# A list of further expert tiles, and the second attention entered tile by tile

## What is computed

```python
for i in range(DEPTH):
    hl = xl * (1.0 + sc1_l) + sh1_l
    # i == 0: window attention on 256 tokens and 256 of context; i == 1: differential attention
    xl = layer_norm(DEEPNORM_ALPHA * xl + g1_l * al, ln_attn_g[i], ln_attn_b[i])
    hl2 = xl * (1.0 + sc2_l) + sh2_l
    # the experts: 512 tokens in layer 0 (with context), 256 in layer 1
    xl = layer_norm(DEEPNORM_ALPHA * xl + g2_l * yl, ln_ffn_g[i], ln_ffn_b[i])

def moe_ffn(h, ...):          # 16 experts in 4 groups, two experts of one group for each token
    for e in range(N_EXPERTS):
        y = (jax.nn.silu(h @ w_gate[e]) * (h @ w_up[e])) @ w_down[e]
        out = out + gates[:, e:e + 1] * y
```

## Time and profile before

| | us |
|---|---|
| median of 3 runs | 2689.21 (2688.8 to 2693.2) |
| the profiled execution, its time | 2687.47 |
| its span in the profile | 2685.6 |
| PE busy | 2363.7 (88%) |
| DVE busy | 1625.8 (61%) |
| ACT busy | 1332.1 (50%) |
| POOL busy | 123.0 (5%) |

### The profile page before, as it was taken

How to read it: one execution, slowest core, us unless ns; L and a number is a source line. 1 busy time by engine, 2 the same in 40 slices (tenths; PEclk the granted TensorE clock), 3 DMA queues, 4 the chain that set the end, 5 groups by cost and what they waited for, 6 DMA issues and landing times. The chain is left out here.

```text
span 2685.6 us, 29338 instructions
## 1 busy us (share of the span) xinstructions
PE 2363.7 (88%) x11416; PEld 1886.5 (70%) x11416; DVE 1625.8 (61%) x2313; ACT 1332.1 (50%) x2010; POOL 123.0 (5%) x118
## 2 busy tenths in 40 slices
PE   8999889999999979899889887999938976999963
PEld 6887667888888758788766575777726754877741
DVE  5556245655555535555624577898866477888832
ACT  5555344655555534555324514777722443777720
POOL 0001000000000000000010000000012000000001
PEclk9999889999999979999899997999969987999986
DMA  7664455665665544666324637999953115999963
GB/s 250 235 234 157 173 219 174 206 219 207 230 220 188 173 157 147 222 233 216 116 70 167 217 130 258 378 377 380 360 181 126 49 49 172 376 375 384 380 235 120
DMA packets 175534, 588.04 MB, mean 219 GB/s; under 512 B 14960, under 2 KB 23600, under 8 KB 143632
## 3 DMA queue, kind: packets, MB, share of 16 engines
q1 hardware_dynamic: 153120, 503.95, 53.0%
q10 hardware_dynamic: 15632, 57.87, 5.4%
q0 software_dynamic: 6624, 24.12, 2.4%
HBM read 538.62 MB, written 47.28 MB: 218 GB/s over the span
## 5 line engine op out<-in xcount | busy, mean ns | idle before, releaser
L315 DVE TENSOR_TENSOR LO<-RAW,HI 128x1024 fp32r<-128x1024 f32 x558 | 659.8, 1220 | 222.6 <-ACT HI L301 220.9
L301 ACT ACTIVATE HI<-RAW 128x1024 fp32r<-128x1024 f32 x558 | 568.5, 1053 | 366.6 <-PE PS L373 191.5
L371 PE MATMUL PS<-HI,FR 128*128 128x512 f32 (+2 forms) x1808 | 699.1, 387 | 36.9 <-DVE LO L315 16.3
L373 PE MATMUL PS<-HI,FR 128*128 128x512 f32 (+2 forms) x1808 | 691.4, 382 | 0.0
L372 PE MATMUL PS<-LO,FR 128*128 128x512 f32 (+2 forms) x1808 | 690.6, 382 | 0.0
L301 ACT ACTIVATE HI<-RAW,SM 128x512 fp32r<-128x512 f32 (+2 forms) x576 | 360.4, 681 | 309.5 <-PE PS L373 159.5
L317 DVE SCALAR_TENSOR_TENSOR LO<-RAW,SM,HI 128x512 fp32r<-128x512 f32 (+2 forms) x576 | 378.8, 709 | 212.1 <-ACT HI L301 212.0
L371 PEld LDWEIGHTS PS<-HI,FR 128*128 128x128 f32 x1808 | 344.9, 191 | 110.6 <-DVE LO L315 20.8
L373 PEld LDWEIGHTS PS<-HI,FR 128*128 128x128 f32 x1808 | 344.3, 190 | 66.2
L372 PEld LDWEIGHTS PS<-LO,FR 128*128 128x128 f32 x1808 | 345.1, 191 | 62.5
L435 ACT ACTIVATE FR<-PS 128x512 fp32r<-128x512 f32 x224 | 122.4, 587 | 236.7 <-PE PS L416 218.6
(11 more groups left out here) (296 smaller groups left out, 2275.9 us busy)
## 6 DMA issues: line engine op xcount, KB each, us to landing
RAW<-in_w_ffn_in SPq DMA_DIRECT2D x88, 1024.0 KB, 5.2
RAW<-in_w_gate SPq DMA_DIRECT2D x68, 1024.0 KB, 7.8
RAW<-in_w_up SPq DMA_DIRECT2D x68, 1024.0 KB, 7.3
RAW<-in_w_down SPq DMA_DIRECT2D x64, 1024.0 KB, 8.5
RAW<-in_w_ada SPq DMA_DIRECT2D x48, 1024.0 KB, 4.9
RAW<-in_w_ffn_out SPq DMA_DIRECT2D x44, 1024.0 KB, 5.1
RAW<-in_w_in SPq DMA_DIRECT2D x44, 1024.0 KB, 5.1
YD<-CN ACTq DMA_DIRECT2D x24, 1024.0 KB, 5.1
```

Source lines behind the costliest of these rows:

```text
L301: e.activation(HI[:, i % NSPLIT, c], raw_of(j)[:, c], ACT.Copy, scale=1.0 if g is None else g).then_inc(*hi_done.up())
L315: e.tensor_tensor(LO[:, i % NSPLIT, c], raw_of(j)[:, c], hi, ALU.subtract).then_inc(*lo_done.up())
L371: e.matmul(o, h, hi[:, j, :], start=first and k + j == 0, stop=False)
L373: x = e.matmul(o, ll, hi[:, j, :], start=False, stop=end)
```

## The change

The further tiles come from a list. `dve_list` finds, in every layer, the up to eight pairs of expert and level whose tile is needed, in ascending order, and writes four things for each: whether it is there (`CNT` 0 to 7), its expert (8 to 15), its first row in `YD` (16 to 23), and the token indices of its places (`IDX` 72 to 79). `further` is a nest of at most `MORE` = 7 conditions in layer 0 and 3 in layer 1. The loads of weights and the store address memory by a register. "The tile before it" is now the one before it in the list. SP's wait for PE moves into the taken branch. The list comes after `dve_weights`, the maximum over the experts is gone, and the counts are no longer converted in `dve_route`.

At the end of layer 0, the norms of tiles 2 and 3 move before the further tiles. ACT and DVE split the first parts of `wqkv_b_2` there too, before the additions. DVE modulates tile 0 before the gate and addition of tile 1, and PE turns and projects tile 0 before it turns tile 1. The additions of tiles 2 and 3 move behind the second part of block 0 and the third of block 1 on DVE, and before `hi_parts` of block 0 on ACT.

```diff
+        MORE = [7, 3]
+        def dve_list(e, q, l):
+            s, n = f"m{l}", 16 * (X_TILES[l] - 1)
+            cf, tokens = x_s2[:, 32:48], PS[bank[f"{s} tokens"]][:, 16:16 + n]
+            key, col, step, top = x_y1[:, 0:n], x_y1[:, 64:72], x_y1[:, 72:88], x_y1[:, 96:104]
+            same = x_y1[:, 512:512 + 8 * n].rearrange("p (i c) -> p i c", i=8)
+            over = x_y1[:, 128:128 + n]
+            for j in range(1, X_TILES[l]):
+                e.tensor_scalar(over[:, 16 * j - 16:16 * j], cf, float(P * j), None, ALU.is_gt).then_inc(*dve.up())
+            e.tensor_scalar(key, C["iota"][:, 16:16 + n], -1.0, 64.0, ALU.mult, ALU.add).then_inc(*dve.up())
+            q.wait_ge(*dve.last())
+            e.tensor_tensor(key, key, over, ALU.mult).then_inc(*dve.up())
+            q.wait_ge(*dve.last())
+            e.max(top, key).then_inc(*dve.up())
+            q.wait_ge(*dve.last())
+            e.tensor_scalar(col, top, -1.0, 64.0, ALU.mult, ALU.add).then_inc(*dve.up())
+            e.tensor_copy(CNT[:, 0:8], top).then_inc(*dve.up())
+            q.wait_ge(*dve.last())
+            e.tensor_scalar(CNT[:, 16:24], col, float(P), None, ALU.mult).then_inc(*dve.up())
+            for j in (2, 3):
+                e.tensor_scalar(step[:, 8 * j - 16:8 * j - 8], col, 16.0 * j, 16.0, ALU.is_ge, ALU.mult).then_inc(*dve.up())
+            e.tensor_tensor(same, C["iota"][:, 16:16 + n].unsqueeze(1).to_broadcast([P, 8, n]),
+                            col.unsqueeze(2).to_broadcast([P, 8, n]), ALU.is_equal).then_inc(*dve.up())
+            q.wait_ge(*dve.last())
+            e.tensor_tensor(same, same, tokens.unsqueeze(1).to_broadcast([P, 8, n]), ALU.mult).then_inc(*dve.up())
+            e.scalar_tensor_tensor(step[:, 0:8], col, -16.0, step[:, 0:8], ALU.add, ALU.subtract).then_inc(*dve.up())
+            q.wait_ge(*dve.last())
+            e.tensor_tensor(CNT[:, 8:16], step[:, 0:8], step[:, 8:16], ALU.subtract).then_inc(*dve.up())
+            e.reduce_sum(col, same, AX).then_inc(*dve.up())
+            q.wait_ge(*dve.last())
+            e.tensor_copy(IDX[:, 72:80], col).then_inc(*dve.up(f"{s} list"))
+        def further(e, q, l, mine, one, first=None, end=None, i=0):
             n0, met = [c.n for c in mine], dict(q.met)
-            value = load_count(e, k) if counted is None else counted[k]
-            with e.If(value > limit):
-                body()
+            with e.If(e.value_load(CNT[0:1, i:i + 1], min_val=0, max_val=64) > 0):
+                if first:
+                    first()
+                one(i, f"m{l} more {i}", f"m{l} more {i - 1}" if i else None)
+                if i + 1 < MORE[l]:
+                    further(e, q, l, mine, one, i=i + 1)
+                if end:
+                    end()
             with e.Else():
...
# act_further
-                r = (j * NE + k) * P
-                e.dma_start(YD[r:r + P, :], x_y[0]).then_inc(*more_yd.up(by=16))
+                row = e.value_load(CNT[0:1, 16 + i:17 + i], min_val=NE * P, max_val=(X_TILES[l] * NE - 1) * P)
+                e.dma_start(YD[bass.ds(row, P), :], x_y[0]).then_inc(*more_yd.up(by=16))
# pool_further
-                if more_before(l, j, k):
-                    q.wait_ge(*more_pe.at(f"{more_before(l, j, k)} xT"))
+                if prev:
+                    q.wait_ge(*more_pe.at(f"{prev} xT"))
# sp_further
+                k = e.value_load(CNT[0:1, 8 + i:9 + i], min_val=0, max_val=NE - 1)
...
-                                    A[w][l, k].rearrange("(p k) c -> p k c", p=P)[:, 4 * i:4 * i + 4, :]).then_inc(
+                                    A[w][l, bass.ds(k, 1)].rearrange("e (p k) c -> p (e k) c", p=P)[
+                                        :, 4 * h:4 * h + 4, :]).then_inc(*landed.up(by=16))
...
-            for landed in (more_gate, more_up, more_down):
-                q.wait_ge(*landed.last())
-            q.wait_ge(*more_pe.at(f"m{l} all"))
+            def end():
+                for landed in (more_gate, more_up, more_down):
+                    q.wait_ge(*landed.last())
+                q.wait_ge(*more_pe.at(f"m{l} all"))
# act_moe
             act_further(e, q, l)
+            if l == 0:
+                hi_parts(e, q, of["qb p0"][0])
# dve_route
-            e.reduce_max(cf[:, 16:17], cf[:, 0:16], AX).then_inc(*dve.up())
...
-            e.tensor_copy(CNT[:, :], cf).then_inc(*dve.up(f"{s} counts"))
# dve_moe
             dve_weights(e, q, l)
+            dve_list(e, q, l)
...
-            dve_norms(e, q, f"o{l}", ("o0 again", "o1")[l], (0, 1))
+            dve_norms(e, q, f"o{l}", ("o0 again", "o1")[l], O_TILES[l])
             dve_further(e, q, l)
+            if l == 0:
+                lo_parts(e, q, of["qb p0"][0])
+                dve_add_up(e, q, 0, 0)
+                dve_add_results(e, q, 0, 1)
+                dve_modulate_b(e, q, 0)
+                dve_add_gated(e, q, 0, 1, 0)
+                dve_hidden_lo(e, q, "qb", 0)
+                dve_add_gated(e, q, 0, 1, 1)
+                dve_stats(e, q, "m0", 1)
+                dve_modulate_b(e, q, 1)
+                dve_hidden_lo(e, q, "qb", 1)
# pe_attn_b
-            pe_hidden_T(e, q, s, (0, 1), b_hid, rot)
...
+                    if blk == 0:
+                        pe_hidden_T(e, q, s, (t,), b_hid, rot2)
# act_attn_b
-            hi_parts(e, q, of[f"{s} p0"][0])
+            for t in (2, 3):
+                act_add_up(e, q, 0, t)
...
-                if blk < 2:
-                    act_add_up(e, q, 0, 2 + blk)
# dve_attn_b
-                if blk < 2:
-                    dve_norms(e, q, "o0", "o0 again", (2 + blk,))
-                    dve_add_up(e, q, 0, 2 + blk)
-                for m in of[f"{s} p{blk}"]:
+                for i, m in enumerate(of[f"{s} p{blk}"]):
+                    if (blk, i) in ((0, 2), (1, 3)):
+                        dve_add_up(e, q, 0, 2 + blk)
                     lo_parts(e, q, m)
```

More of the change, by code:

```diff
@@ L1871, in pe_places @@
             x.then_inc(*pe.up(f"{s} tokens"))
-            freed[b] = [(dve, f"{s} index")]
+            freed[b] = [(dve, f"{s} list")]
         def dve_places(e, q, l):
@@ L1923, in where_over @@
             q.met = met
-        def load_count(e, k):
-            return e.value_load(CNT[0:1, k:k + 1], min_val=0, max_val=512)
-        def further(e, q, l, j, mine, first, one, early=False, counted=None):
-            def body():
-                held = counted
-                if j == 1:
-                    first()
-                    if early:
-                        held = [load_count(e, k) for k in range(NE)]
-                for k in range(NE):
-                    where_over(e, q, k, P * j, mine, lambda: one(k, j, f"m{l} more {j} {k}"), held)
-                if j + 1 < X_TILES[l]:
-                    further(e, q, l, j + 1, mine, first, one, early, held)
-            where_over(e, q, NE, P * j, mine, body)
         def pe_further(e, q, l):
@@ L1946, in first, with one @@
                     pe_free(q, b)
[L1948 removed]
+            def one(i, s, prev):
                 q.wait_ge(*more_xg.at(f"{s} x"))
[L1950 to L1951 removed]
+                for k, b in enumerate(every(x_g[0], 8) + every(x_g[0], 8, 4)):
+                    x = e.matmul(PS[k // 4][:, P * (k % 4):P * (k % 4) + P], b, ident, start=True, stop=True,
                                  is_transpose=True)
@@ L1966, in one @@
                 q.wait_ge(*more_down.at(f"{s} w"))
-                if more_before(l, j, k):
-                    q.wait_ge(*more_act.at(f"{more_before(l, j, k)} y in"))
+                if prev:
+                    q.wait_ge(*more_act.at(f"{prev} y in"))
                 for h in range(2):
-                    for i in range(4):
-                        x = e.matmul(PS[5 + h][:, :], x_p[1][:, P * i:P * i + P],
-                                     half_of(more_w[i], h), start=i == 0, stop=i == 3)
+                    for k in range(4):
+                        x = e.matmul(PS[5 + h][:, :], x_p[1][:, P * k:P * k + P],
+                                     half_of(more_w[k], h), start=k == 0, stop=k == 3)
                 x.then_inc(*more_pe.up(f"{s} y"))
-            q.wait_ge(*dve.at(f"m{l} counts"))
-            further(e, q, l, 1, [more_pe], first, one)
+            q.wait_ge(*dve.at(f"m{l} list"))
+            further(e, q, l, [more_pe], one, first)
             more_pe.also(f"m{l} all")
@@ L1994, in one @@
                 q.wait_ge(*more_act.last())
-                r = (j * NE + k) * P
-                e.dma_start(YD[r:r + P, :], x_y[0]).then_inc(*more_yd.up(by=16))
-            q.wait_ge(*dve.at(f"m{l} counts"))
-            further(e, q, l, 1, [more_act, more_yd], first, one, True)
+                row = e.value_load(CNT[0:1, 16 + i:17 + i], min_val=NE * P, max_val=(X_TILES[l] * NE - 1) * P)
+                e.dma_start(YD[bass.ds(row, P), :], x_y[0]).then_inc(*more_yd.up(by=16))
+            q.wait_ge(*dve.at(f"m{l} list"))
+            further(e, q, l, [more_act, more_yd], one, first)
```

(21 more changed lines are left out.)

91 lines of the change are left out of this document (45 added, 46 removed).

## The result

The changed kernel takes 2653.48 us (median of 4 runs, 2651.8 to 2660.7), against 2689.01 (4 runs, 2681.1 to 2693.2) for the kernel before on the same chip: ratio 0.9874, 95% interval 0.9855 to 0.9893. In a second set (6 runs against 17 of the kernel before) it was 2655.93 against 2689.59, ratio 0.9867, 0.9844 to 0.9890. The forecast was 2661 with a range of 2652 to 2672: 28.1 us less were forecast, 34 to 36 came, and 2653.48 lies near the low edge. The changed kernel itself ran in the first two sets only, so where a later experiment is compared with it, the steps of the profiles count, not the totals.

The account below looks back on a forecast made before the run. Skips waiting on PE's walk bounded layer 1's further tiles, and DVE's pace the second attention's entry. Gains of 0.8, 17.4 and 9.9 us made 28.1 off 2687.5, 2659.4; adjusted to the runs' median, 2661, range 2652 to 2672.

Parts of the forecast that it names:

- The list: Routing: dve_list hides in DVE's idle time, some 4.6 us in layer 0; two instructions leave the path, 0.8 us gained.
- The further tiles: Layer 1's end: the gap between two tiles closes and thirteen skips become one, 17.4 us gained, bounds 13 and 19.
- a cold start behind the gap: Layer 1's second further tile: it takes 28.9 us and would become as short as the first, 27.6.
- F to G: Layer 1: ACT's copy of expert 15 to its copy of the second further tile; both tiles forecast at 27.6 us.
- G to H: Layer 1's end: ACT's copy of the second further tile to POOL taking results; thirteen skips become one, POOL 0.9 later.
- The entry: Layer 0's end into the second attention: earlier start and less DVE work, 9.9 us gained, bounds 4 and 14.
- A to D: Layer 0: ACT's copy of expert 15 to DVE scaling the queries, closing the second attention's entry; 9.9 us gain forecast.
- A to B: Layer 0: ACT's copy of expert 15 to DVE's first addition; forecast 2.7 us earlier, bounds 0 and 5.4.
- The second part: From DVE's first addition to PE turning tiles 2 and 3, norms and low parts moved away: 8.1 us gained.
- the entry gives nothing: Second attention's entry: DVE stays the bound, gathers meet extra loads, new waits eat the gain; 2671 us, chance 0.14.
- the second tile waits for its weights: Layer 1: the down load may come 5 to 8 us late if register addresses slow it; 2667 us, chance 0.08.
- The branch becomes cheap: Layer 0's end: ACT's branch over seven bodies nears the short ones, gathers start at 1965.2; 2656 us, chance 0.18.

Follow-up runs that it names:

- held tile: Changed kernel, but the second further tile's gather and its gate and up loads wait for the first tile's last product: 2666.61 us, ratio 0.9914.
- second profile of before: The kernel before, without an edit, in a second profiled execution: 2688.53 us.
- the entry alone: Kernel before with the new entry to the second attention, keeping old counts and the old walk over sixteen experts: 2681.45 us, ratio 0.9964.
- the two loads out of the way: Changed kernel, but SP sends four wqkv_b loads early and holds two until the first two gathers land: 2653.60 us, ratio 0.9856.
- the list alone: Kernel before with the list, register addresses and SP's moved wait, keeping the old entry to the second attention: 2659.48 us, ratio 0.9886.
- late splits: Changed kernel, but ACT splits five parts and DVE four only after hidden tile 0 is turned: 2656.86 us, ratio 0.9879.

## Why the prediction was right, and where it was short

**The list** was hidden, as said. DVE's timeline in the routing, the list's dearest instructions and the first one behind it:

```profile
1637.86 0.21 DVE L1918 MAX8 SC<-SC 128x8 f32<-128x48 f32 x1
...
1638.67 0.55 DVE L1926 TENSOR_TENSOR SC<-CN,SC 128x384 f32<-128x384 f32 x1
1639.26 0.56 DVE L1929 TENSOR_TENSOR SC<-SC,PS 128x384 f32<-128x384 f32 x1
...
1643.01 0.69 DVE L439 TENSOR_TENSOR FR<-PS,FR 128x512 fp32r<-128x512 f32 x1 [2.25 <-ACT FR L435]
```

It took 3.6 us (1637.17 to 1640.76) instead of 4.6, and 2.25 us of waiting are left behind it. The two instructions off the path gave 0.4 us in layer 0 (24.0 to 23.6 from the first instruction of the routing on DVE, 1617.19 and 1619.4, to the first gathered low half).

**The further tiles** are the term that was too small, by 1.5 us. 17.4 us were forecast for F to H; the two profiles of each kernel give 81.0 and 82.3 before, 61.9 and 63.5 after, so 18.9. The gap of 11.6 was right, and "a cold start behind the gap", 1.3 us, was the step that failed: it took 27.6 us as the price of a tile at full clock. That first tile had itself run in part at the lower clock (0.90 in the mean). Its 32 gate and up products took 15.61 us where they take 14.00 at 1.00, and the second tile's 16.08, with transposes of 1.97 instead of 1.04: 4.6 us of clock in the two. How much of that is lost again differs by execution: the ten profiles with the new list and no held tile show F to G at 53.1 or 53.2 (six), at 54.8 (one) and at 56.2 to 56.5 (three), as one of the tiles' products or two take 1.4 to 1.7 us more. That the changed kernel's first profile lost nothing is therefore no property of the change. F to G was forecast to fall by 13.6 us (the gap, the cold start and the start's 0.75) and fell by 17.0 in both pairs. That SP's earlier gate load "gives nothing" held in the profile it was read from; in the second profile of before, and in the entry alone, the first tile waited 1.3 and 0.9 us more for it.

Behind the tile the step went the other way: from G to H 3.7 us were forecast (4.3 of skips less the register's 0.6), 1.9 came. The store lands late. The profile's answer on its line, two issues in each kernel, the last one being the shorter; first the kernel before, then the changed one:

```profile
DMA to landing us min/median/max: 4.4/7.6/10.7
```

```profile
DMA to landing us min/median/max: 5.9/7.1/8.4
```

SP's timeline in the changed kernel has what is new beside it:

```profile
2617.66 0.35 SPq L1283 DMA_DIRECT2D GB<-in_ln_ffn_g  x1
2618.06 0.43 SPq L1283 DMA_DIRECT2D GB<-in_ln_ffn_b  x1
```

In the kernel before the same two loads leave at 2668.4 and 2668.8, 20 us behind the store. SP no longer skips experts with PE, so they now run beside it, at 245 GB/s from issue to landing against 123. The last store landed after 4.0 to 4.4 us in the three profiles with the old walk and after 5.8 to 6.1 in those with the list. That the two loads cost these 1.5 us is argued from this, it wasn't tried.

**The entry** was forecast at 9.9 us and is 10.7 and 8.3 in the two profiles from A to D, 9.5 in the mean. Its first part, 2.7 us from A to B, came out at 2.7 and 3.1, but by luck: two errors cancel. I took the middle of two bounds twice. The branch did become cheap: from A to the first gather it is 6.1 us where it was 9.1, 3.0 instead of 1.3 us earlier. That is the rival's time, but its mechanism is not all of it: with the same short branch and SP's loads beside the store it is 9.4. And the gathers gained nothing: 10.7 and 11.3 us from gather to addition, where 9.1 was forecast and 10.4 stood before. The Trainium skill (DMA: Bandwidth & Descriptors, Queues, rings and completion order) has it that a DMA engine takes turns between its queues packet by packet, by which the 10.45 us would stay. The case agrees with it: with the two loads out of the way it is 8.2 us here and 7.6 in the kernels with the list alone or with late splits. A second cause was not forecast. The first two gathers took POOL 3.5 us to issue beside DVE's splits (1966.36 to 1969.85), where they took 2.2 in the kernels without splits there; with the loads held the same 3.5 us of issue go with 8.2 instead of 7.6, so it is worth about 0.6 us, the loads 2.5. The second part, 8.1 us, was 7.8 in one profile and 5.5 in the other; the second shows PE's clock down at block 2's first tile (0.79 us for a matmul that takes 0.50 at full clock), which the forecast had as half a chance of 2 us.

**Of the rivals**, "the entry gives nothing" (2671) is refuted by the 8.3 to 10.7 us; "the second tile waits for its weights" too: PE's timeline has no wait for a load there, and four issues by a register's expert took 0.33 to 0.47 us each at the queue. "The branch becomes cheap" (2656) was right in its place and nearest in its total, but that nearness owes more to the 4 to 6 us that stay open below than to the branch. The Trainium skill (Runtime: NRT & Kernel Launch, Instruction fetch mechanics) puts such a wait down to a target outside the fetched window. From the end of the copy, 1.86 us against 6.8 before and 7.62 in the entry alone, which jumps over the old walk, agree; which length decides no run here shows.

**What stays open.** The resolved steps add up to 0.4 + 18.9 + 9.5, some 29 us, and perhaps 0.4 more for layer 1's routing and 0.6 behind POOL's take (28.1 to 27.5). So the forecast's sum of 28.1 is close to what the steps show. The medians differ by 34 to 36, with intervals of the ratios that reach down to 29 and 30 us. The remaining 4 to 6 us may in part be noise; in the profiles they lie in stretches with the same code: the first routing is reached 2 to 3 us earlier on average in the eleven profiles with the new list than in the three with the old counts (1618 against 1621), layer 1's experts take some 2 us less (329 against 331). Spreads of 5 to 11 us and three profiles on one side don't make a cause of it, and no experiment here was aimed at it.

## What to carry over

A step that POOL or SP makes only when another engine walks past it is paid twice, as a gap and in PE's clock behind it; here 11 us of gap cost 15 to 16.7. When work is moved under a gather, ask what its consumption lets the load queue send: the early splits filled idle time of their engine, and the two loads that they let through took more than half of their worth back (2.1 us left of 5.5). An engine that is 85% busy on the path is not yet full: work that was due anyway, put where DVE waited for PE's turn, gave another 5.8 us.

## What the runs showed of the hardware that was not expected

- What PE's clock costs differs by execution. The same 32 matmuls took 14.00 us at a granted clock of 1.00, 15.6 to 15.7 at 0.89 to 0.90, and 16.85 at 0.83. Behind a gap of 11 us they took 16.1 to 16.9 in every profile, without one 14.0 to 16.5; the first further tile of the changed kernel had the full clock in one execution and 0.89 in the next.
- Gathers beside plain loads: from the first gather to the first addition 7.6 us with the early loads done before, 8.2 to 8.7 with two loads held and DVE's splits beside, 10.4 to 11.3 with loads running at a DMA share of 0.82 to 1.05.
- POOL beside a working DVE: its 128x512 addition took 2.19 us during a low part and 1.27 while DVE waited (the profile's spans on POOL are rough); its instruction for a gather 1.1 to 2.0 us beside the splits and 0.94 without.
- From the end of ACT's copy to its next step it was 1.86 us over seven bodies, 6.8 and 7.62 over the 48.
- A store of 0.5 MB to HBM, from issue to landing: 4.0 to 4.4 us at the end of layer 1 with at most a DMA share of 0.35 beside it, 5.8 to 6.1 beside two gain loads; at the end of layer 0 4.4 to 8.7 us with four loads of `wqkv_b` sent at about the same time.
- MAX8 on 128x48 elements took 0.21 us, like any other narrow instruction of DVE; DVE instructions with 384 columns took 0.55.
